# One up slab by eight products, another order of the first two slabs, and copies and joins ahead of splits, in a two-block transformer kernel

## The chip, the core and the metric

The kernel runs on one core of a Trainium2 chip. The metric is the device time of one execution in microseconds (us); lower is better. The engines are TensorE (PE; its weight loads are PEld), VectorE (DVE), ScalarE (ACT), GpSimd (POOL) and SyncE (SP, which here only issues DMAs). Each has its own in-order instruction queue, and they meet only at semaphores: an instruction that waits holds up everything behind it on its engine.

## The reference, cut to what matters

Two blocks are computed one after the other on 512 tokens of width 1024, all in float32. The change touches three products of them:

```python
# first block, entry
h = rmsnorm(x, norm_mix_pre); proj = h @ w_in          # the first two slabs of w_in
# first block, MLP (width 4096)
f = relu(h @ w_up) ** 2; y = f @ w_down
# second block, end
h = rmsnorm_2(x, norm_ffn_2)
x = x + (silu(h @ w_ffn_gate_2) * (h @ w_ffn_up_2)) @ w_ffn_down_2   # width 2816
```

## The kernel before

**Slabs.** Every weight matrix is read in slabs of 1024 x 256 (two column blocks of 128; 1 MB). Float32 accuracy is had by splitting each operand into a high and a low float32r part: ACT copies raw to `hi`, then DVE (for the first slab POOL) subtracts raw - hi into `lo`. A product is then three matmuls per 128 deep tile: hi by hi, hi by input-low, lo by input-hi. A slab by eight products is 2 blocks x 8 tiles x 3 = 48 matmuls of 512 tokens, summed in two of the four `gemm` banks (`G`).

**Seven products.** Most slabs of the MLP's up matrix (`up4` to `up15`) and of the second block's gate and up matrices (`fgate1`.. and `fup1`..) are multiplied in Strassen-Winograd form: seven products, each 4 pairs x 3 = 12 matmuls of 256 tokens, 84 in all, in the order 1, 6, 7, 5, 2, 4, 3. They go through the four `misc` banks (`M`) in turn, so product number n waits until the bank of number n-4 has been read (`p_read`). They need sums of weight quarters, made by POOL in four operations (`weight_sums`, `ffn_sums`), a split of the slab in three parts (`even`, `sums`, `odd`, each a `hi` on ACT and a `lo` on DVE), a copy of product 1 out of its bank (`copy_p1` on ACT), and seven joins on DVE (`join_u2`, `join_u3`, `join_u4_c22`, `join_c11_c21`, `join_c12`). For the gate slabs there follow a scaling by RSTD (`scale`), tanh on ACT, `silu` on DVE, another RSTD factor on POOL (`norm_gate`), and `gated` on DVE.

**Order.** Nothing is planned at run time: each engine's program is written out by hand, in the loop `for w in range(1, N_W)` for the second block's end. Slab numbers there, counted from `fgate0`: `fgate0` 0, `fup0` 1, `fgate1` 2, `fup1` 3, `fgate2` 4, `fup2` 5, then a down slab (`fpart2`) 6. Slabs 0 and 1 are done by eight products (`first_gate`, `up_block`), 2 to 5 by seven. A raw buffer (three of them) is loaded again when the slab three before is done, a `hi` buffer (two) is free when the slab two before is done, and the buffers of weight sums are two.

**Entry.** SP issues the four quarters of x and then slab 0 in two DMAs (columns 0 to 127 and 128 to 255). ACT squares x, copies two transposed tiles (L1527), waits for both halves of slab 0, makes `w_hi` in one operation (L1492, called as `split_hi(0)`) and then the eight `h_hi` tiles (L1500). POOL waits for `hi_done` and makes `w_lo` in eight operations (L3194), with one increment after the last. PE's `first_slab` (L671, L676) does 16 matmuls w_hi by h_hi in the order in which h_hi comes, waits for all of `w_lo`, does 16 w_lo by h_hi, then 16 w_hi by h_lo. DVE starts h_lo (L2271) when `w_lo` is there, and makes slab 1's low part behind it (`split_lo(1)`, L2212). Slab 1 is an ordinary `slab`: it waits for its low part before its first matmul.

**MLP.** For u in 4 to 15, ACT and DVE first make parts of the next slab and then copy and join products of slab u. `up14` is the one with another seven-product slab on both sides (`paired and closed`).

Of the kernel before, what the change touches and what calls it, by code (L numbers as in the profile page):

```python
# [25 lines left out]
P = 128  # L26
# [88 lines left out]
def build(nc, a, out):  # L115
# [115 lines left out]
    PIECES = [4 if PH["nsa"][0] + 3 <= s < PH["nsa"][0] + 5 else 3 if PH["branch2"][0] <= s < PH["branch2"][0] + 4 or s == PH["small"][0] else 2  # L231
# [191 lines left out]
    SEVENS = [W_SLAB[w] + n for w in range(1, N_W) for n in range(2)]  # L423
# [13 lines left out]
    def joined_at(n, x):  # L437

        return S("joined"), JOINED_0 + 8 * ((n + 1) // 2) + 7 * (n // 2) + x
# [33 lines left out]
    def _(sp):  # L473
# [158 lines left out]
    def _(pe):  # L632
# [26 lines left out]
        def first_slab(s, blocks, hi_base, lo_base):  # L659

            m = BLOCKS_BEFORE[s]
            pe.wait_ge(S("hi_done"), s + 1)
            for b in range(blocks):
                pe.wait_ge(evac[(m + b) % 4], (m + b) // 4 + 1)
            for w in (hi_of, lo_of):
                if w is lo_of:
                    pe.wait_ge(S("lo_done"), s + 1)
                for k in range(KT):
                    pe.wait_ge(S("hhi_ready"), hi_base + k + 1)
                    for b in range(blocks):  # L670
                        nc.tensor.matmul(G[(m + b) % 4][:], w(s)[:, k, P * b:P * b + P], HHI[:, k, :],  # L671
                                         start=k == 0 and w is hi_of, stop=False)
            for b in range(blocks):
                for k in range(KT):
                    pe.wait_ge(S("hlo_ready"), lo_base + k + 1)
                    mm = nc.tensor.matmul(G[(m + b) % 4][:], hi_of(s)[:, k, P * b:P * b + P], HLO[:, k, :],  # L676
                                          start=False, stop=k == KT - 1)
                mm.then_inc(S("block_full"), 1)

        def run(name, hi, lo, kts=range(KT), ready=None, lo_slab=0, slabs=None, new_h=None):  # L680
            s0, n, _, _ = PH[name]
            n = slabs or n
            for s in range(s0 + lo_slab, s0 + lo_slab + n):
                if new_h and s == s0 + lo_slab:
                    first_slab(s, 2, *new_h)
                else:
                    slab(s, hi, lo, kts, ready)
# [29 lines left out]
        pe.wait_ge(S("inv_ready"), 1)  # L717
# [53 lines left out]
        mm.then_inc(S("ln_var"), 1)  # L771
# [4 lines left out]
        mm.then_inc(S("ln_spread"), 1)  # L776
# [359 lines left out]
        for hd in range(GLA_H):  # L1136
            nc.tensor.matmul(take((hd + 1) % 4)[:], ONE32[32 * hd:32 * hd + 32, :], RS4[32 * hd:32 * hd + 32, :],
                             start=True, stop=True).then_inc(S("gla_rstd_full"), 1)
# [10 lines left out]
        mm.then_inc(S("hidden_full"), 1)  # L1149
# [240 lines left out]
        for w in range(1, N_W):  # L1390
            for n in (2 * w - 2, 2 * w - 1):
                for p in ORDER[1 if n == 0 else 0:]:
                    product(n, p)
# [72 lines left out]
    def _(act):  # L1466
# [49 lines left out]
        act.wait_ge(S("eps_ready"), 1)  # L1516
# [11 lines left out]
        split_hi(0)  # L1528
# [59 lines left out]
        act.wait_ge(S("ln_var"), 1)  # L1588
# [161 lines left out]
        for u in range(FIRST7, N_UP):  # L1750
            s = PH[f"up{u}"][0]
            paired, closed = s + 1 in UP_AT, s - 1 in UP_AT
            if paired:
# [3 lines left out]
            up_copy(u)  # L1757
# [192 lines left out]
        act.wait_ge(S("hidden_full"), 1)  # L1950
        A_(HT[:], M[2][:, 0:P], ACT.Tanh, scale=0.5).then_inc(S("hidden_tanh"), 1)
# [161 lines left out]
        def gate_tanh(w, b):  # L2113

            act.wait_ge(*joined_at(2 * w - 2, SCALED_AT))
            A_(SQ[b][:], FGATE[:, b, :], ACT.Tanh, scale=0.5).then_inc(S("ffn_tanh"), 1)

        def act_hi(w, b):

            if w:  # L2120
                act.wait_ge(S("ffn_gated"), 2 * w - 1 + b)
            else:
                act.wait_ge(*evac_at(PH["fup0"][2] + b))
# [7 lines left out]
        for w in range(1, N_W):  # L2131
            f_ = W_SLAB[w]
            even_hi(f_ + 1)
            copy_p1(2 * w - 2)
            if w <= 2:
                if w == 2:
                    act_hi(w - 1, 0)
                act_hi(w - 1, 1)
            sums_hi(f_ + 1)
            odd_hi(f_ + 1)  # L2140
            if f_ + 2 in SEVEN_OF:
                even_hi(f_ + 2)
# [54 lines left out]
    def _(dve):  # L2197
        V = nc.vector
        V.memset(EPSB[:], EPS).then_inc(S("eps_ready"), 1)
        for n in (128, 512):  # L2200
            V.memset(INV[n][:], 1.0 / n)
        V.memset(INV[1024][:], 1.0 / 1024).then_inc(S("inv_ready"), 1)
# [174 lines left out]
        dve.wait_ge(S("ln_spread"), 1)  # L2377
# [1036 lines left out]
```

## Time and profile before

| | us |
|---|---|
| median of 3 runs | 1400.23 (1400.18 to 1402.51) |
| the profiled execution's own time | 1401.67 |
| its span | 1399.5 |
| PE busy | 1379.1 (99% of the span) |
| DVE busy | 1020.1 (73%) |
| ACT busy | 615.1 (44%) |
| POOL busy | 419.4 (30%) |

The span is what the trace covers, from the first instruction to the last; the execution's own time is 2.2 us more. The TensorE clock granted was 0.998 of full over the span. Times in rows are counted from the span's start. A matmul's row has a start and a length; matmuls overlap, so the step from one start to the next is what one costs, not its length.

### The profile page before, as it was taken

Reading aid. Unit: us, or ns where it says so; the run is one execution under the profiler, and the core shown is the slowest. Engines: PE = TensorE matmul, PEld = TensorE weight load, DVE = VectorE, ACT = ScalarE, POOL = GpSimd, SP = SyncE. Lnnn points to the kernel's source line nnn. Section 1 sums busy time; section 2 is a strip of 40 time slices with the busy share of each in tenths; the row PEclk is TensorE's granted clock in tenths of the full one; section 3 lists DMA queues with packets and bytes.
Section 4 is the critical chain, followed back from the end, with each engine's and each line's share of the span. In section 5 each row is a group of like instructions: output and inputs, shape, how many; then the busy total and the mean of one; then the engine's idle time right before and its main releaser. Section 6 shows DMA issues by size and latency. Waiting matters only on the chain.

```text
span 1399.5 us, 20853 instructions
## 1 busy us (share of the span) xinstructions
PE 1379.1 (99%) x8375; PEld 1176.2 (84%) x8375; DVE 1020.1 (73%) x1490; ACT 615.1 (44%) x905; POOL 419.4 (30%) x311
## 2 busy tenths in 40 slices
PE   7999999999999999999999999999999999999998
PEld 6888788988988999888878776668888899999997
DVE  6998774757776687578474666774579999998983
ACT  6223344646333434346453437662355343433434
POOL 1040014101333234121132711111235654455532
PEclk9999999999999999999999999999999999999999
DMA  6322223303323323423244212111323232332322
GB/s 201 119 91 91 91 90 124 118 0 96 116 91 92 120 91 100 119 91 98 90 91 121 74 61 61 31 31 61 120 63 94 86 121 91 109 103 91 121 68 83
DMA packets 125792, 129.89 MB, mean 93 GB/s; under 512 B 15777, under 2 KB 110945, under 8 KB 125665
## 3 DMA queue, kind: packets, MB, share of 16 engines
q1 hardware_dynamic: 124560, 124.90, 28.5%
q0 software_dynamic: 992, 3.47, 0.8%
q8 instruction: 67, 1.10, 0.3%
q14 instruction: 29, 0.23, 0.0%
q10 hardware_dynamic: 144, 0.20, 0.0%
HBM read 126.06 MB, written 2.10 MB: 92 GB/s over the span
## 4 chain that ended last, share of the span: by engine, by line
PE 90%; DVE 4%; ACT 2%; issue 2%; POOL 1%; DMA 1%; SPq 0%; ACTq 0%; DVEq 0%; POOLq 0%
PE gemm L643 30%; PE misc L1314 13%; PE gemm L916 9%; PE misc L902 8%; PE gemm L1343 6%; PE gemm L762 3%; PE gemm L1219 2%; PE gemm L930 2%; PE gemm L1357 2%; PE misc L1240 2%; PE misc L1259 1%; PE gemm L846 1%; PE gemm L793 1%; PE gemm L1232 1%; PE misc L1067 1%
## 5 line engine op out<-in xcount | busy, mean ns | idle before, releaser
L643 PE MATMUL gemm<-h_hi,w_hi 128*128 128x512 f32 x520 | 205.0, 394 | 0.0
L643 PE MATMUL gemm<-h_hi,w_lo 128*128 128x512 f32 x520 | 202.5, 389 | 0.0
L643 PE MATMUL gemm<-h_lo,w_hi 128*128 128x512 f32 x520 | 202.5, 389 | 0.0
L2212 DVE TENSOR_TENSOR w_lo<-w_raw,w_hi 128x2048 fp32r<-128x2048 f32 x45 | 103.6, 2303 | 68.8 <-ACT w_hi L1492 68.7
L643 PEld LDWEIGHTS gemm<-h_hi,w_hi 128*128 128x128 f32 x520 | 97.6, 188 | 23.2 <-issue 2.4
L643 PEld LDWEIGHTS gemm<-h_hi,w_lo 128*128 128x128 f32 x520 | 97.6, 188 | 20.4
L643 PEld LDWEIGHTS gemm<-h_lo,w_hi 128*128 128x128 f32 x520 | 97.7, 188 | 19.9 <-issue 0.2
L1492 ACT ACTIVATE w_hi<-w_raw 128x2048 fp32r<-128x2048 f32 x50 | 95.5, 1910 | 5.4 <-PE gemm L762 3.2
L1314 PE MATMUL misc<-ffn_in_hi,ffn_hi 128*128 128x256 f32 x320 | 90.9, 284 | 4.2 <-ACT copy_p L2111 2.6
L1314 PE MATMUL misc<-ffn_in_lo,ffn_hi 128*128 128x256 f32 x320 | 90.5, 283 | 0.0
L1314 PE MATMUL misc<-ffn_in_hi,ffn_lo 128*128 128x256 f32 x320 | 90.5, 283 | 0.0
L2302 DVE SCALAR_TENSOR_TENSOR conv_out<-v_padded,conv_cols,conv_out 128x512 f32<-128x512 f32 x120 | 89.8, 807 | 0.5
L3242 POOL TENSOR_TENSOR mlp_sums<-mlp_raw 128x512 f32<-128x512 f32 x12 | 22.2, 1852 | 211.3 <-DMA mlp_raw<-in_w_up 202.9
L916 PE MATMUL gemm<-f_hi,mlp_hi 128*128 128x512 f32 x192 | 74.8, 389 | 0.0
L916 PE MATMUL gemm<-f_lo,mlp_hi 128*128 128x512 f32 x192 | 74.8, 389 | 0.0
L916 PE MATMUL gemm<-f_hi,mlp_lo 128*128 128x512 f32 x192 | 74.7, 389 | 0.0
L3229 POOL TENSOR_TENSOR sq_sum<-sq_sum,sq 128x512 f32<-128x512 f32 (+1 forms) x27 | 39.2, 1453 | 103.3 <-ACT sq L2029 51.4
L1314 PE MATMUL misc<-ffn_in_hi,ffn_sums_hi 128*128 128x256 f32 x240 | 68.1, 284 | 0.4 <-DVE ffn_up L3007 0.4
L2048 ACT ACTIVATE ffn_hi<-ffn_raw 128x1024 fp32r<-128x1024 f32 x20 | 21.2, 1061 | 106.7 <-POOL ffn_raw L3360 77.9
L1314 PE MATMUL misc<-ffn_in_lo,ffn_sums_hi 128*128 128x256 f32 x240 | 67.9, 283 | 0.0
L1314 PE MATMUL misc<-ffn_in_hi,ffn_sums_lo 128*128 128x256 f32 x240 | 67.9, 283 | 0.0
L3368 POOL TENSOR_TENSOR ffn_gate<-ffn_gate,rstd 128x512 f32<-128x512 f32 x20 | 30.8, 1557 | 119.1 <-DVE ffn_gate L3055 119.1
(608 smaller groups left out, 4058.2 us busy)
## 6 DMA issues: line engine op xcount, KB each, us to landing
w_raw<-in_w_in SPq DMA_DIRECT2D x62, 512.0 KB, 4.6
mlp_raw<-in_w_down SPq DMA_DIRECT2D x32, 512.0 KB, 4.6
mlp_raw<-in_w_up SPq DMA_DIRECT2D x26, 512.0 KB, 4.7
ffn_raw<-in_w_ffn_gate SPq DMA_DIRECT2D x22, 512.0 KB, 4.7
ffn_raw<-in_w_ffn_up SPq DMA_DIRECT2D x22, 512.0 KB, 4.4
ffn_raw<-in_w_ffn_down SPq DMA_DIRECT2D x16, 512.0 KB, 4.3
w_raw<-in_w_o SPq DMA_DIRECT2D x8, 512.0 KB, 4.0
w_raw<-in_w_out SPq DMA_DIRECT2D x8, 512.0 KB, 4.0
```

The costliest lines, as they stand in the source:

```text
L643: mm = nc.tensor.matmul(bank[:], w(s)[:, kt, col0:col0 + P], x(n), start=first, stop=last)
L762: mm = nc.tensor.matmul(G[m % 4][:], wide(w(s0 + j))[:, k, P * b:P * b + P], x[:, k, :], start=k == 0 and n == 0, stop=k == 3 and n == 2)
L902: mm = nc.tensor.matmul(up_bank(u, p)[:, 0:HALF], w, x, start=pair == 0 and n == 0, stop=pair == 3 and n == 2)
L916: mm = nc.tensor.matmul(G[m % 4][:], wide(w(s))[:, k, P * b:P * b + P], x(4 * c + k), start=k == 0 and n == 0, stop=k == 3 and n == 2)
L930: mm = nc.tensor.matmul(G[m % 4][:], w(s)[:, k, P * b:P * b + P], x(3 * KT + k), start=n == 0, stop=n == 23)
L1314: mm = nc.tensor.matmul(bank[:, 0:HALF], w_, x[:, a_, pair, :], start=pair == 0 and i == 0, stop=pair == 3 and i == 2)
L1343: mm = nc.tensor.matmul(G[m % 4][:], wide(w)[:, k, P * b:P * b + P], x[:, e, :], start=k == 0 and n == 0, stop=k == 3 and n == 2)
L1492: nc.scalar.activation(part(hi_of(s), s), part(raw_of(s), s), ACT.Copy).then_inc(S("hi_done"), SLABS_AT[s])
L2212: V.tensor_tensor(part(lo_of(s), s), part(raw_of(s), s), f(part(hi_of(s), s)), SUB).then_inc(S("lo_done"), SLABS_AT[s])
L2302: ins = V.scalar_tensor_tensor(y, x, w, y, MUL, ADD)
L3229: Q.tensor_tensor(SQA[:, cols], SQA[:, cols], SQ[j % 2][:, cols], ADD).then_inc(S("sq_added"), 1)
L3368: Q.tensor_tensor(FGATE[:, b, :], FGATE[:, b, :], RSTD[:], MUL).then_inc(S("gate_normed"), 1)
```

## The change

Four things, and a renaming of semaphores (`eps_ready`, `inv_ready` to `fills_ready`; `ln_var`, `ln_spread` to `ln_full`; `gla_rstd_full`, `hidden_full` to `late_full`; `r_tanh`, `hidden_tanh` to `branch_tanh`) with counts to match.

1. `fup1` is done by eight products (`up_block(1, 0)`, `up_block(1, 1)`, in `G` banks) instead of seven. POOL makes no sums for it, its split is one `down_hi` and one `down_lo` (whole slab), there are no joins for it; `first_silu` and `first_gated` take over for w = 1. The loops of ACT and DVE get a branch for w = 1 in which `copy_p1` comes ahead of the splits. On POOL the sums of `fgate2` come directly behind those of `fgate1`.
2. Slab 0: its first half has a semaphore of its own and a `w_hi` copy of its own; POOL increments after each low tile; PE takes the low products of tile k-1 right behind the high ones of tile k, and the h_lo products tile by tile for both blocks.
3. Slab 1 (`second_slab`): all products with w_hi first, for both blocks, those with w_lo last.
4. MLP: for `up4` the copy and the joins u2, u3 come ahead of the next slab's split; for `up14` the odd part's low split comes behind the joins c11 and c21.

```diff
-        FFN_PHASES += [(f"fgate{w}", 1, 0 if w else 2), (f"fup{w}", 1, 0 if w else 2)]
+        FFN_PHASES += [(f"fgate{w}", 1, 0 if w else 2), (f"fup{w}", 1, 0 if w > 1 else 2)]
...
-    SEVENS = [W_SLAB[w] + n for w in range(1, N_W) for n in range(2)]
+    SEVENS = [W_SLAB[w] + n for w in range(1, N_W) for n in range(2) if w + n != 2 or n == 0]
...
+            if c == 0:
+                dst, src = sides.pop(0)
+                sp.dma_start(dst, src).then_inc(S("first_side"), 16)
...
+        def first_slab():
+            def lows(k):
+                pe.wait_ge(*((S("first_lo"), k + 1) if k < KT - 1 else (S("lo_done"), 1)))
+                for b in range(2):
+                    nc.tensor.matmul(G[b][:], lo_of(0)[:, k, P * b:P * b + P], HHI[:, k, :], start=False, stop=False)
+            for k in range(KT):
+                pe.wait_ge(S("hhi_ready"), k + 1)
+                for b in range(2):
...
+                    nc.tensor.matmul(G[b][:], hi_of(0)[:, k, P * b:P * b + P], HHI[:, k, :], start=k == 0, stop=False)
+                if k:
+                    lows(k - 1)
+            lows(KT - 1)
+            for k in range(KT):
+                pe.wait_ge(S("hlo_ready"), k + 1)
+                for b in range(2):
+                    mm = nc.tensor.matmul(G[b][:], hi_of(0)[:, k, P * b:P * b + P], HLO[:, k, :], start=False, stop=k == KT - 1)
...
+        def second_slab():
+            pe.wait_ge(S("hi_done"), 2)
...
+            for w, x in ((hi_of, HHI), (hi_of, HLO), (lo_of, HHI)):
+                if w is lo_of:
+                    pe.wait_ge(S("lo_done"), 2)
+                for b in range(2):
+                    for k in range(KT):
...
-        split_hi(0)
+        act.wait_ge(S("first_side"), 16)
+        nc.scalar.activation(hi_of(0)[:, :, 0:P], raw_of(0)[:, :, 0:P], ACT.Copy).then_inc(S("first_hi"), 1)
+        act.wait_ge(*raw_full(0))
+        nc.scalar.activation(hi_of(0)[:, :, P:SLAB], raw_of(0)[:, :, P:SLAB], ACT.Copy).then_inc(S("hi_done"), 1)
...
@@ scalar, the second block's end @@
+            if w == 1:
+                copy_p1(GATE_N[w])
+                act_hi(0, 1)
+                down_hi(f_ + 1)
+                even_hi(f_ + 2)
+                gate_tanh(w, 0)
+                gate_tanh(w, 1)
+                sums_hi(f_ + 2)
+                odd_hi(f_ + 2)
+                act_hi(1, 0)
+                continue
...
@@ vector, MLP @@
+            if u == FIRST7:
+                up_u2(u)
+                up_u3(u)
...
-            if paired:
+            if paired and not closed:
                 up_odd_lo(u + 1)
             up_c11(u)
             up_c21(u)
+            if paired and closed:
+                up_odd_lo(u + 1)
...
@@ vector, the second block's end @@
+                first_gated(0, 1)
                 act_lo(0, 0)
+                join_u2(gate)
+                act_lo(0, 1)
+                join_u3(gate)
+                down_lo(f_ + 1)
+                join_u4_c22(gate)
+                join_c11_c21(gate)
+                join_c12(gate)
+                scale(w)
+                even_lo(f_ + 2)
+                first_silu(w, 0)
+                first_silu(w, 1)
+                sums_lo(f_ + 2)
+                first_gated(w, 0)
+                odd_lo(f_ + 2)
+                continue
+            if w == 2:
+                first_gated(1, 1)
+                act_lo(1, 0)
             even_lo(f_ + 1)
...
@@ gpsimd @@
-        ins.then_inc(S("lo_done"), 1)
+            ins.then_inc(S("first_lo") if k < KT - 1 else S("lo_done"), 1)
...
         weight_sums(0)
-        for w in range(1, N_W):
-            weight_sums(2 * w - 1)
-            if W_SLAB[w] + 2 in SEVEN_OF:
-                weight_sums(2 * w)
+        weight_sums(1)
+        for w in range(2, N_W):
+            weight_sums(UP_N[w])
```

## Rows read from the trace of the kernel before

**Rows 1.** The page, part 1: busy time of each engine, share of the span.
```profile
PE 1379.1 (99%) x8375; PEld 1176.2 (84%) x8375; DVE 1020.1 (73%) x1490; ACT 615.1 (44%) x905; POOL 419.4 (30%) x311
```
**Rows 2.** Timeline of the entry: start us, us, engine, line, what, [idle before <-releaser].
```profile
2.67 8.02 SPq L507 DMA_DIRECT2D w_raw<-in_w_in  x4
12.78 1.91 ACT L1492 ACTIVATE w_hi<-w_raw 128x2048 fp32r<-128x2048 f32 x1 [1.16 <-DMA w_raw<-in_w_in]
14.59 5.02 ACT L1500 ACTIVATE h_hi<-h_T 128x512 fp32r<-128x512 f32 x8
14.76 5.62 POOL L3194 TENSOR_TENSOR w_lo<-w_raw,w_hi 128x256 fp32r<-128x256 f32 x8 [13.82 <-ACT w_hi L1492]
15.35 5.05 PE L671 MATMUL gemm<-h_hi,w_hi 128*128 128x512 f32 x16 [2.52 <-ACT h_hi L1500]
20.41 4.90 DVE L2271 TENSOR_TENSOR h_lo<-h_T,h_hi 128x512 fp32r<-128x512 f32 x8 [1.47 <-POOL w_lo L3194]
20.43 3.93 PE L671 MATMUL gemm<-h_hi,w_lo 128*128 128x512 f32 x16
27.86 0.48 PE L643 MATMUL gemm<-h_hi,w_hi 128*128 128x512 f32 x1
```
**Rows 3.** DMA issues from 2.6 to 3.1 us: count, KB, us to landing.
```profile
w_raw<-in_w_in SPq DMA_DIRECT2D x1, 512.0 KB, 8.3
```
**Rows 4.** Timeline of ACT: one copy of 128x1024.
```profile
1048.99 1.05 ACT L2048 ACTIVATE ffn_hi<-ffn_raw 128x1024 fp32r<-128x1024 f32 x1
```
**Rows 5.** Timeline of PE: first and last of 48 matmuls, at 512 and at 256 tokens.
```profile
1037.04 0.39 PE L1368 MATMUL gemm<-ffn_in_hi,ffn_hi 128*128 128x512 f32 x1
...
1047.69 0.39 PE L1368 MATMUL gemm<-ffn_in_hi,ffn_lo 128*128 128x512 f32 x1
...
1060.55 0.28 PE L1314 MATMUL misc<-ffn_in_hi,ffn_hi 128*128 128x256 f32 x1
...
1066.18 0.28 PE L1314 MATMUL misc<-ffn_in_hi,ffn_sums_lo 128*128 128x256 f32 x1
```
**Rows 6.** Timeline of DVE: a whole slab's low part, that of slab 8.
```profile
97.68 2.28 DVE L2212 TENSOR_TENSOR w_lo<-w_raw,w_hi 128x2048 fp32r<-128x2048 f32 x1
```
**Rows 7.** Timeline of DVE and PE at the turn from up14 to up15.
```profile
557.43 1.21 DVE L2543 TENSOR_TENSOR mlp_lo<-mlp_raw,mlp_hi 128x1024 fp32r<-128x1024 f32 x1
...
559.11 0.36 PE L902 MATMUL misc<-mlp_in_sums_hi,mlp_sums_hi 128*128 128x256 f32 x1 [0.29 <-DVE relu L2548]
```
**Rows 8.** Timeline of PE, 1040 to 1110 us: all matmuls that waited.
```profile
1067.49 0.35 PE L1314 MATMUL misc<-ffn_in_hi,ffn_hi 128*128 128x256 f32 x1 [1.03 <-ACT copy_p L2111]
1084.27 0.35 PE L1314 MATMUL misc<-ffn_in_hi,ffn_sums_hi 128*128 128x256 f32 x1 [0.42 <-DVE ffn_up L3007]
1090.43 0.36 PE L1314 MATMUL misc<-ffn_in_hi,ffn_hi 128*128 128x256 f32 x1 [1.62 <-ACT copy_p L2111]
1094.39 0.35 PE L1314 MATMUL misc<-ffn_in_hi,ffn_hi 128*128 128x256 f32 x1 [0.64 <-DVE join_u L3007]
1096.88 0.36 PE L1314 MATMUL misc<-ffn_in_hi,ffn_hi 128*128 128x256 f32 x1 [0.83 <-DVE ffn_gate L3007]
```
**Rows 9.** Timeline of ACT around the first and third of these waits.
```profile
1065.49 0.63 ACT L2124 ACTIVATE ffn_act_hi<-ffn_up 128x512 fp32r<-128x512 f32 x1 [7.06 <-DVE ffn_up L3062]
...
1066.98 0.37 ACT L2111 ACTIVATE copy_p<-misc 128x256 f32<-128x256 f32 x1
...
1088.96 1.06 ACT L2048 ACTIVATE ffn_hi<-ffn_raw 128x1024 fp32r<-128x1024 f32 x1 [6.62 <-POOL ffn_raw L3360]
```
**Rows 10.** The page, part 6: a gate slab's DMAs, us to landing.
```profile
ffn_raw<-in_w_ffn_gate SPq DMA_DIRECT2D x22, 512.0 KB, 4.7
```
**Rows 11.** By line: duration ns min/median/max, first and last start us.
```profile
L3358 POOL TENSOR_TENSOR ffn_sums<-ffn_raw x20: 1290/1416/2677, 1043.0 to 1329.9; 128x512 f32<-128x512 f32 x20
L3048 DVE SCALAR_TENSOR_TENSOR ffn_gate<-sq,ffn_gate x2: 1776/1780/1783, 1057.8 to 1061.2; 128x512 f32<-128x512 f32 x2
L3055 DVE SCALAR_TENSOR_TENSOR ffn_gate<-sq,ffn_gate x20: 679/683/995, 1079.4 to 1351.0; 128x512 f32<-128x512 f32 x20
```

More of the change, by code:

```diff
@@ L422, in build @@
     W_SLAB = [PH[f"fgate{w}"][0] - SF for w in range(N_W)]
-    SEVENS = [W_SLAB[w] + n for w in range(1, N_W) for n in range(2)]
+    SEVENS = [W_SLAB[w] + n for w in range(1, N_W) for n in range(2) if w + n != 2 or n == 0]
+    GATE_N, UP_N = [[SEVENS.index(W_SLAB[w] + n) for w in range(2, N_W)] for n in range(2)]
+    GATE_N, UP_N = [None, 0] + GATE_N, [None, None] + UP_N
+    JOINS_TO = [sum(7 if x in UP_N else 8 for x in range(n)) for n in range(len(SEVENS))]
     SEVEN_OF = {f_: n for n, f_ in enumerate(SEVENS)}
@@ new lines, in second_slab @@
+        def second_slab():
+            pe.wait_ge(S("hi_done"), 2)
+            for b in range(2):
+                pe.wait_ge(evac[2 + b], 1)
+            for w, x in ((hi_of, HHI), (hi_of, HLO), (lo_of, HHI)):
+                if w is lo_of:
+                    pe.wait_ge(S("lo_done"), 2)
+                for b in range(2):
+                    for k in range(KT):
+                        mm = nc.tensor.matmul(G[2 + b][:], w(1)[:, k, P * b:P * b + P], x[:, k, :],
+                                              start=k == 0 and w is hi_of and x is HHI, stop=k == KT - 1 and w is lo_of)
+                    if w is lo_of:
+                        mm.then_inc(S("block_full"), 1)
@@ L681, in run @@
+        def run(name, hi, lo, kts=range(KT), ready=None, lo_slab=0, slabs=None):
             s0, n, _, _ = PH[name]
@@ L683, in run @@
             for s in range(s0 + lo_slab, s0 + lo_slab + n):
[L684 to L687, printed above, removed]
+                slab(s, hi, lo, kts, ready)
         def mean_rows(src, start, stop, bank=M[0]):
@@ L1137, in _ @@
             nc.tensor.matmul(take((hd + 1) % 4)[:], ONE32[32 * hd:32 * hd + 32, :], RS4[32 * hd:32 * hd + 32, :],
-                             start=True, stop=True).then_inc(S("gla_rstd_full"), 1)
+                             start=True, stop=True).then_inc(S("late_full"), 1)
         gate_block(3)
@@ L1390, in _ @@
         for w in range(1, N_W):
-            for n in (2 * w - 2, 2 * w - 1):
-                for p in ORDER[1 if n == 0 else 0:]:
-                    product(n, p)
+            for n in (GATE_N[w], UP_N[w]):
+                if n is None:
+                    up_block(1, 0)
+                    up_block(1, 1)
+                else:
+                    for p in ORDER[1 if n == 0 else 0:]:
+                        product(n, p)
             if 2 <= w < N_W - 1:
@@ L3009, in joined_into @@
         def joined_into(n):
-            return FUP if n % 2 else FGATE
+            return FUP if n in UP_N else FGATE
         def join_u2(n):
```

149 lines of the change are left out of this document (62 added, 87 removed).

## The prediction

> **What bounds the kernel now.** I read the page's part 1 first: PE is busy for 1379.1 of 1399.5 us and the next engine for 73% [rows 1]. So an edit pays only where it shortens PE's list of matmuls or takes away a stop of PE. Next I read what a matmul costs, as the step between starts: 48 matmuls of 512 tokens start within 47 steps from 1037.04 to 1047.69, so 0.2266 us each; at 256 tokens it is 47 steps from 1060.55 to 1066.18, 0.1198 us each [rows 5]. A slab by eight products is thus 48 x 0.2266 = 10.88 us and one by seven products 84 x 0.1198 = 10.06 us. Then I looked for PE's stops in the timeline, in the three places that the change touches.
>
> Entry: PE's first matmul of slab 0 is at 15.35, the first of slab 1 at 27.86; 48 matmuls take 12.5 us instead of 10.9, because the first 16 follow h_hi (5.05 us for 16) and the next 16 wait for the last of POOL's eight low tiles [rows 2]. MLP: one stop, at 559.11 [rows 7]. Second block's end: five stops between 1067 and 1097 [rows 8], and none after; they are the start-up of the seven-product pipeline.
>
> **Part A, entry.** ACT is free at 12.78 - 1.16 = 11.62 and waits until 12.78 for slab 0 [rows 2]. The first of its two DMAs is issued at 2.67 [rows 2] and lands 8.3 us later, at 10.97 [rows 3]. So the first half copy starts at 11.62, and takes 1.05 us [rows 4]; the second starts at 12.78, when the second DMA is there as before, and ends at 13.83. Before, the whole copy took 1.91 and h_hi began at 14.59; now h_hi 0 begins near 13.75 and POOL at 13.9 instead of 14.76 (0.86 earlier). The split in two costs ACT 0.2 us more, hidden in the 1.16 us of waiting; uncovered, it would be 0.2 us later. Later h_hi tiles gain less: the last ended at 19.61, and h_T comes from DVE; I give them 0.1 us.
>
> PE then: h_hi 0 is there at 14.4, so the start is 14.5. Each tile is now four matmuls, 0.91 us, slower than POOL's pace of 5.62/8 = 0.70 and h_hi's of 5.02/8 = 0.63 [rows 2]. Only tile 3 is late (h_hi 3 at about 16.97, where PE would be at 16.96), nothing else. Thirty-two matmuls are 7.25 us, with two small waits 22.0. Sixteen more follow with h_lo: 3.63 us, to 25.7. DVE starts h_lo when POOL is done, 13.9 + 5.62 = 19.5, and needs 4.90: the last at 24.5, PE wants it at 25.2. So slab 1 can start at 25.75 instead of 27.86: **2.1 us**. Bounds: if nothing comes earlier from ACT, PE starts at 15.35, waits 0.15 more for h_hi 1 and ends at 15.95 + 30 x 0.2266 + 3.63 = 26.4, a gain of 1.5; if there are no waits at all from 14.5, 14.5 + 10.88 = 25.4, a gain of 2.5.
>
> What would be late next is slab 1's low part: DVE makes it behind h_lo, until 24.5 + 2.3 = 26.8 (2.28 for such a part [rows 6]). The old order would have waited there 1.1 us; the new one has 32 matmuls with w_hi first and wants it at 33.0. Its first column block is complete 16 x 0.2266 = 3.6 us later than before, its second at the same point; the ACT and DVE work behind it on their queues waits for the second anyway. Farther on DVE runs the convolution, and its low parts come on time by about 4 us: that of slab 8 is done at 97.68 + 2.28 = 99.96, while PE reaches slab 8 at 27.86 + 7 x 10.88 = 104.0 [rows 2, 5, 6]. A PE that is 2.1 us earlier doesn't use that up. No stop takes the gain back.
>
> **Part B, MLP.** At up15's second product PE stood for DVE's join of up14; ahead of that join lay the odd low part, 1.21 us from 557.43 [rows 7]. Moved behind two joins, it is done at 559.3, and up15's product 2 wants it at 563. The stop is gone: 0.29 by its row, 0.45 us against the pace. I take **0.45**, ends 0.2 and 0.5. The same edit for up4 costs and gives nothing: it puts a whole split (1.9 on ACT, 2.28 on DVE) behind the third product, and the four products that are left (5.8 us) cover it; without that cover it would cost up to its 2.28 us of low part.
>
> **Part C, second block's end.** Matmuls: 10.88 instead of 10.06, so +0.82 us. Stops: I follow PE from 1066.30, when product 5 of fgate1 has been issued.
>
> - Copy of product 1: ACT made the act_hi tile until 1066.12, then the even part for fup1, then the copy [rows 9]. Now the copy comes second, done at 1066.4. PE resumes at 1066.55 instead of 1067.49 and ends fgate1 (three products, 4.32 us) at 1070.9.
> - fup1 needs one low part of the whole slab. ACT copies it from 66.95 to 68.85 (1.9). On DVE the low part (2.28) stands behind act_lo 0, u2, act_lo 1, u3. Here POOL matters. fgate2's raw slab may be loaded when fup0 is done, 1060.55, and lands 4.7 after its issue [rows 5, 10], so POOL's four sums start at about 1065.4 and no longer at 1072. In the rows, the DVE product of two SBUF tiles takes 0.68 us when alone (L3055) and 1.78 when it ran beside POOL (L3048), and a POOL sum 1.29 at best and up to 2.68 [rows 11]. Taken in turns, each waits for the other's whole operation, some 1.1 to 1.2 us. In turns I get act_lo 0 at 67.2, act_lo 1 at 68.95, POOL's third sum to 70.15, the low part to 72.3. PE starts fup1 at 72.4: a new stop of 1.5 us. It ends at 83.3.
> - In these 10.9 us DVE does five joins (0.33 each), two scalings, fgate2's even low part, four silu steps and the sums' low part (1.75): 74.0, 75.2, 76.4, then in turns with POOL's sums for fup2 (its raw slab lands at about 75.4) silu to 83.4, sums to 85.1. fgate2's second product wants this at 84.75: a stop of 0.45. Its product 1 copy, stood before behind fup2's even high part, and this behind POOL's sums for fup2, made late (ACT idle 6.62 until 1088.96 [rows 9]). They are now made by about 1079 to the part that it needs: the 1.62 stop is gone. The joins u2 (89.6) and u3 (90.5) come before 90.9 and 92.4, C22 (92.95) before 93.8.
> - fgate2 so takes 10.06 + 0.45, from 83.3 to 93.85, where fup2 started at 1096.88 [rows 8]. **3.0 us** earlier, with the 0.82 in it.
>
> Bounds: no collisions between DVE and POOL, then fup1 starts at 1071.2, fup2 at 1092.1, gain 4.8. If the three last stops of [rows 8], 3.1 us by the rows, stay for want of DVE time, the gain is zero to 0.5. Nothing that is queued later gets more work.
>
> The collision itself is also what the Trainium skill says ("SBUF — State Buffer", Who interferes with whom): a DVE instruction with two SBUF inputs and a GpSimd instruction that reads SBUF exclude each other for their whole length, and which was issued first decides. The rows agree (1.78 against 0.68 us). Read without it, the sum of part C would be 4.8, with it 3.0.
>
> **Sum.** 2.1 + 0.45 + 3.0 = 5.55 us. The profiled execution took 1401.67, so it would be 1396.1; this is 1.44 above the median of 1400.23, and the median after is then 1394.7.
>
> **Rivals.**
>
> 1. *No collisions.* POOL's earlier sums fall into DVE's waits; C is 4.8, the sum 7.35, time 1392.9. For it: the joins, with one operand in PSUM, don't collide. Against: the four silu steps lie just where fup2's sums run.
> 2. *The stops move on.* in my working of part C DVE has no idle time at all from 1066 to 1094, so any slip goes to PE; fup1's start and fgate2's second and fifth products wait as long as the old ones: C is 0.5, sum 3.0, time 1397.2.
> 3. *The entry doesn't pass on.* The convolution on DVE takes its slack back, or h_hi is no earlier: A is 0 to 0.5, sum 3.7, time 1396.5. Against: 4 us of slack.
> 4. *Slower.* DVE's silu chain ahead of fgate2's `sums_lo`: if each of the five POOL operations beside it holds DVE for its longest 2.68 us (instead of about 1.15), the sums come 5 x 1.53 = 7.65 us later, at 1092.75, PE stops 8.0 instead of 0.45, and C is -4.55: sum -2.0, time 1402.2. It decides from 5.55 us of lateness, 2.3 us per POOL operation. Against: 2.68 contains POOL's own waiting, and 1.29 is its length alone [rows 11].
>
> **How the numbers follow.** Forecast 50%, rival 1 20%, rival 2 14%, rival 3 11%, rival 4 5%. Range: the forecast's own bounds are 1393.5 to 1396; toward both sides I go to 1392.0 (rival 1 with the entry's better end) and 1397.8 (rival 2 with the worse). A measurement of this kernel tells 0.2% (2.8 us) from no change: faster than 1397.4 are the forecast, rivals 1 and 3, and half of rival 2, 0.88, of which I keep 0.86; within, half of rival 2 and part of rival 4: 0.11; slower 0.03.
>
> **What would show it.** Slab 1's first matmul at 25.75 (25.4 to 26.4), the first of slab 0 near 14.5. No wait at up15. fup1 (then `up_block`) starting 1.5 us after fgate1's last product, behind DVE's whole low part; fgate2's second product behind the sums' low part; fup2 starting 3.0 us earlier relative to fup0's end. Sections between them with unchanged lengths. It would be wrong if a stop longer than 0.5 us appeared in the convolution stage, or if the stops in fgate2 were still over 3 us.

## The result, and the profile after

| us | before | after |
|---|---|---|
| median | 1400.30 (1400.18 to 1402.51, 4 runs) | 1391.61 (1391.17 to 1392.80, 4 runs) |
| the profiled execution's own time | 1401.67 | 1391.79 |
| its span | 1399.5 | 1389.9 |
| first matmul of slab 1 | 27.86 | 26.37 |
| first matmul of `up4` | 337.45 | 335.95 |
| first matmul of `fgate1` | 1060.55 | 1056.94 |
| first down matmul (L1343, after L1367) | 1107.05 | 1098.07 |
| start of the last nine matmuls | 1392.78 | 1383.99 |

The ratio is 0.9936, 95% interval [0.9918, 0.9953]: 9.0 us less (6.6 to 11.5), where 5.55 was forecast and 1392.0 was the lower end of the range. (The medians of the table differ by 8.7.) In the text below, "us less" beside a ratio is what the ratio makes of 1400. Busy times after, from the page's part 1 [rows 1]:

```profile
PE 1375.9 (99%) x8339; PEld 1173.7 (84%) x8339; DVE 1015.8 (73%) x1483; ACT 614.0 (44%) x903; POOL 404.6 (29%) x305
```

**Where the 9.9 us between the two profiled executions went.** I take PE's position from one stage to the next. Up to slab 1 it gained 1.49 us, though in this execution the setup data landed 0.55 later (PE's first matmul at 5.44 instead of 4.89), so the entry itself is 2.04 shorter. The convolution added 0.01. The MLP gave 0.52. Between 816 and 820 us there are 1.57 us that no edit gave: the kernel before ran there at a granted clock of 0.57, that after at 1.00 (see the last section). From `fgate1` to the first down matmul it is 46.50 before and 41.13 after, 5.37 less, of which a later stage takes 0.19 back. From the last matmuls to the end of the span it is 0.8 less, and 0.3 lies outside the spans. The edits' own part is thus 2.04 + 0.52 + 5.18 = 7.7 us.

That the entry may be counted from PE's first matmul is borne out by the other traces. Where the clock was full, the five with the new entry have 20.84 to 20.93 us from there to slab 1, though the first matmul stood anywhere from 4.90 to 5.97. The traces with the old entry have 22.97 (the kernel before) and 22.61 (the second block's end alone), so the 2.04 is 1.7 to 2.1.

Entry, timelines of ACT, POOL, DVE and PE after; the columns are as in [rows 2]:

```profile
11.77 1.06 ACT L1557 ACTIVATE w_hi<-w_raw 128x1024 fp32r<-128x1024 f32 x1
12.95 1.06 ACT L1559 ACTIVATE w_hi<-w_raw 128x1024 fp32r<-128x1024 f32 x1
14.18 1.95 ACT L1528 ACTIVATE h_hi<-h_T 128x512 fp32r<-128x512 f32 x3 [0.17 <-DVE h_T L2304]
16.88 3.27 ACT L1528 ACTIVATE h_hi<-h_T 128x512 fp32r<-128x512 f32 x5 [0.76 <-DVE h_T L2304]
...
14.08 5.63 POOL L3247 TENSOR_TENSOR w_lo<-w_raw,w_hi 128x256 fp32r<-128x256 f32 x8 [13.14 <-ACT w_hi L1559]
...
24.57 2.28 DVE L2249 TENSOR_TENSOR w_lo<-w_raw,w_hi 128x2048 fp32r<-128x2048 f32 x1
...
22.71 3.79 PE L687 MATMUL gemm<-h_lo,w_hi 128*128 128x512 f32 x16
26.34 0.27 PE L747 MATMUL misc<-setup_rows 124*128 124x124 f32 x1
26.37 0.94 PE L701 MATMUL gemm<-h_hi,w_hi 128*128 128x512 f32 x3
```

h_hi comes in two groups. Tiles 4 to 8 wait for DVE's h_T and end at 20.15 (before: 19.61, with the setup data 0.55 sooner), so they gained nothing; PE has the low products to do meanwhile.

The second block's end after: the boundaries on PE, then what DVE and POOL did in `fgate1` and `fup1`. None of these matmuls carries a bracket: nothing waited.

```profile
1056.94 0.28 PE L1338 MATMUL misc<-ffn_in_hi,ffn_hi 128*128 128x256 f32 x1
...
1067.01 0.40 PE L1352 MATMUL gemm<-ffn_in_hi,ffn_hi 128*128 128x512 f32 x1
...
1077.92 0.28 PE L1338 MATMUL misc<-ffn_in_hi,ffn_hi 128*128 128x256 f32 x1
...
1098.07 0.40 PE L1367 MATMUL gemm<-ffn_act_hi,ffn_hi 128*128 128x512 f32 x1
```

```profile
1054.21 0.68 DVE L3092 SCALAR_TENSOR_TENSOR ffn_gate<-sq,ffn_gate 128x512 f32<-128x512 f32 x1
1054.93 0.69 DVE L3094 TENSOR_TENSOR ffn_gate<-ffn_gate,rstd 128x512 f32<-128x512 f32 x1
...
1058.00 1.28 DVE L3106 TENSOR_TENSOR ffn_up<-ffn_gate,gemm 128x512 f32<-128x512 f32 x2
...
1061.97 2.29 DVE L3001 TENSOR_TENSOR ffn_lo<-ffn_raw,ffn_hi 128x2048 fp32r<-128x2048 f32 x1
...
1072.68 1.78 DVE L3092 SCALAR_TENSOR_TENSOR ffn_gate<-sq,ffn_gate 128x512 f32<-128x512 f32 x1
1074.50 1.66 DVE L3094 TENSOR_TENSOR ffn_gate<-ffn_gate,rstd 128x512 f32<-128x512 f32 x1
1076.09 2.84 DVE L2990 TENSOR_TENSOR ffn_sums_lo<-ffn_sums,ffn_sums_hi 128x1536 fp32r<-128x1536 f32 x1
...
1062.57 2.85 POOL L3411 TENSOR_TENSOR ffn_sums<-ffn_raw 128x512 f32<-128x512 f32 x1 [17.68 <-DMA ffn_raw<-in_w_ffn_gate]
...
1072.47 1.45 POOL L3411 TENSOR_TENSOR ffn_sums<-ffn_raw 128x512 f32<-128x512 f32 x1 [2.71 <-DMA ffn_raw<-in_w_ffn_up]
```

The reader is to see two things. The collisions that I forecast are there (1.78, 1.66 and 2.84 for operations that take 0.68, 0.69 and 1.75 alone). But the first silu, at 1054.21, took 0.68 where it took 1.78 before [rows 11], and the pair of `first_gated` products begins 1.06 us after `fgate1`'s first matmul. Before, it began 4.23 after it:

```profile
1054.04 2.68 POOL L3358 TENSOR_TENSOR ffn_sums<-ffn_raw 128x512 f32<-128x512 f32 x1 [5.20 <-DVE ffn_in_sums L2970]
1056.80 2.25 POOL L3360 TENSOR_TENSOR ffn_raw<-ffn_raw 128x512 f32<-128x512 f32 x1
...
1064.78 1.28 DVE L3062 TENSOR_TENSOR ffn_up<-ffn_gate,gemm 128x512 f32<-128x512 f32 x2
```

These POOL operations of the kernel before are the sums for `fup1`, which the change takes out. After the change, the low part for `fup1` was done at 1064.3, 2.8 us before PE wanted it.

### The profile page after: what moved, and what is told of

Same layout as the page of the kernel before. It is cut to its first block, busy times and chain, and to the rows that moved or that the text cites. A ratio compares the mean times of both kernels' runs of the same rounds, so it can differ in the third digit from the quotient of the medians.

```text
span 1389.9 us, 20753 instructions
## 1 busy us (share of the span) xinstructions
PE 1375.9 (99%) x8339; PEld 1173.7 (84%) x8339; DVE 1015.8 (73%) x1483; ACT 614.0 (44%) x903; POOL 404.6 (29%) x305
## 4 chain that ended last, share of the span: by engine, by line
PE 96%; DVE 1%; ACT 1%; issue 1%; DMA 0%; ACTq 0%
PE gemm L650 30%; PE misc L1338 14%; PE gemm L940 9%; PE misc L926 9%; PE gemm L1367 6%; PE gemm L786 3%; PE gemm L1243 3%; PE gemm L954 2%; PE gemm L1381 2%; PE misc L1264 2%; PE gemm L1352 2%; PE misc L1283 1%; PE gemm L870 1%; PE gemm L817 1%; PE gemm L701 1%; PE gemm L1392 1%
## 5 line engine op out<-in xcount | busy, mean ns | idle before, releaser
L650 PE MATMUL gemm<-h_hi,w_hi 128*128 128x512 f32 x504 | 198.7, 394 | 0.0
L650 PE MATMUL gemm<-h_hi,w_lo 128*128 128x512 f32 x504 | 196.3, 389 | 0.0
L650 PE MATMUL gemm<-h_lo,w_hi 128*128 128x512 f32 x504 | 196.3, 389 | 0.0
L1338 PE MATMUL misc<-ffn_in_lo,ffn_hi 128*128 128x256 f32 x304 | 86.0, 283 | 0.0
L1338 PE MATMUL misc<-ffn_in_hi,ffn_lo 128*128 128x256 f32 x304 | 86.0, 283 | 0.0
L1338 PE MATMUL misc<-ffn_in_hi,ffn_hi 128*128 128x256 f32 x304 | 86.0, 283 | 0.0
L1338 PE MATMUL misc<-ffn_in_hi,ffn_sums_hi 128*128 128x256 f32 x228 | 64.6, 283 | 0.0
L1338 PE MATMUL misc<-ffn_in_hi,ffn_sums_lo 128*128 128x256 f32 x228 | 64.5, 283 | 0.0
L1338 PE MATMUL misc<-ffn_in_lo,ffn_sums_hi 128*128 128x256 f32 x228 | 64.5, 283 | 0.0
L2540 DVE TENSOR_TENSOR y_T<-y_T,gemm 128x512 f32<-128x512 f32 x46 | 31.4, 683 | 42.6 <-PE gemm L940 30.0
```

The lines of the kernel that those rows point to most:

```text
L650: mm = nc.tensor.matmul(bank[:], w(s)[:, kt, col0:col0 + P], x(n), start=first, stop=last)
L1338: mm = nc.tensor.matmul(bank[:, 0:HALF], w_, x[:, a_, pair, :], start=pair == 0 and i == 0, stop=pair == 3 and i == 2)
L2540: V.tensor_tensor(y, y, G[m % 4][:], ADD).then_inc(evac[m % 4], 1)
```

## The experiments

A useful measure beside the time is the *end stage*: from `fgate1`'s first matmul to the first down matmul, 46.50 us before, 41.13 after. Without a stop it would be 3 x 10.06 + 10.9 = 41.1. A stop *against the pace* is the step from one matmul's start to the next, less the normal step (0.12 us at 256 tokens, 0.23 at 512). One execution's time moves by more than a microsecond for reasons of the clock, so for effects of that size the stage or stop in the trace decides, and the ratio only confirms. The first four kernels ran on one chip, the next four on a second, the last four on a third; across chips the ratios are compared, each to the kernel before on the same chip, and not the times.

**The kernel after again.**

> The changed kernel again, for the size of the whole. From the two traces: entry 2.0 us (1.5 seen, with x's first data 0.55 later in that execution), MLP 0.5, second block's end 5.2, together 7.7 us; the rest of the 8.7 measured (a half-clock stretch of 1.6 us that only the profiled execution of before had, and the last stores landing 0.8 sooner) is taken as chance. If so: 7.7 us less than before, plus or minus 0.5. If something steady is hidden in the rest: 8.5 or more.

1392.64, ratio 0.9943 [0.9930, 0.9955], 8.0 us less. End stage 41.14. The size of the edits' own part, 7.7, holds; this median would have been inside the forecast's range.

**The entry alone** (the kernel before, with slab 0 in halves and interleaved, `second_slab`, and the semaphore names).

> The kernel before with the entry's edits alone (slab 0 in halves, interleaved low weights, slab 1 with w_lo last) and the renamed semaphores. Theory: 2.0 us less than before, slab 1's first matmul 11.5 us after PE's first transpose of x (13.0 before). Rival 3 of the prediction (the entry doesn't pass on): 0 to 0.5 us.

1399.16, ratio 0.9989 [0.9981, 0.9998], 1.5 us less. From PE's first matmul to slab 1 it is 20.91 us, as in the kernel after, so the entry gives what it should. But the MLP takes some of it back (in the profiled execution 0.9 of the 1.0 us that PE was ahead in place):

```profile
PE misc L923 <- DVE up_u L2572: 0.7, 1, 0.7
```

This is PE's list of waits (total, times, longest). The wait is at 344.67, in `up4`, 0.9 us against the pace. In the kernel before the join it waits for was just in time, 0.3 us ahead. PE now comes 1.0 us sooner and DVE does not (the join u2 starts at 344.11, before at 343.94).

**The second block's end alone** (the kernel before, with the `FFN_PHASES`, `SEVENS` and w = 1 edits).

> The kernel before with the second block's end changed alone. Theory (all five stops go and none comes): 6.0 us of stops less 0.82 of matmuls, 5.2 us less than before. The forecast as put: 3.0. If the rest in e0 belongs to this part: 6.

1395.06, ratio 0.9954 [0.9941, 0.9968], 6.4 us less. End stage 41.13, the same as with all edits: it does not depend on the entry.

**GpSimd busy again beside the first silu** (the kernel after; four additional subtractions whose results are overwritten):

```diff
         weight_sums(0)
+        pool.wait_ge(*ffn_raw_full(3))
+        pool.wait_ge(S("ffn_in_part"), PARTS_0 + 4)
+        for i in (0, 1, 2, 0):
+            gstep.inc(Q.tensor_tensor(sums_of(1)[0][:, i, :, :].rearrange("p a n -> p (a n)"), XT[:, 2 * i, :], XT[:, 2 * i + 1, :], SUB))
+            gstep.wait(pool)
         weight_sums(1)
```

> The changed kernel, with four more GpSimd operations of the size and at the place of fup1's weight sums (they subtract tiles of x into the buffer of sums, which is overwritten afterwards). Theory: what the prediction missed is that without fup1's sums GpSimd stands idle beside first_silu, so VectorE reaches fup0's first_gated 3.2 us earlier relative to fgate1's first product. With the four operations back, the silu steps take 1.7 to 1.8 us again, and the stops of the forecast come (1.5 at fup1's start, 0.3 at the copy, 0.5 at fgate2's second product): 2 us more than the changed kernel. Rival (the whole gain is in the other order of ScalarE and VectorE, GpSimd doesn't matter): 0 to 0.3 us more.

1394.02, ratio 0.9951 [0.9938, 0.9963], 1.4 us more than the kernel after beside it (1392.64), where 2 was expected; the intervals overlap, and the trace decides. Timelines of DVE and PE:

```profile
1053.88 1.78 DVE L3092 SCALAR_TENSOR_TENSOR ffn_gate<-sq,ffn_gate 128x512 f32<-128x512 f32 x1
...
1067.97 0.50 PE L1352 MATMUL gemm<-ffn_in_hi,ffn_hi 128*128 128x512 f32 x1 [0.83 <-DVE ffn_lo L3001]
...
1081.25 0.39 PE L1338 MATMUL misc<-ffn_in_hi,ffn_sums_hi 128*128 128x256 f32 x1 [0.64 <-DVE ffn_sums_lo L2990]
```

The silu is back at 1.78, and the stops stand where the prediction had put them: the copy (0.23 us against the pace; forecast 0.25), `fup1`'s start (0.99; 1.5) and `fgate2`'s second product (0.80; 0.45). The end stage is 43.46, 2.3 more than after the change. Against the 46.50 before it is 3.04 less: with POOL busy at this place, part C gives the 3.0 of the forecast.

**GpSimd's sums for `fup1` cut short** (the kernel before, seven products kept; it leaves out most columns of these sums, so that `fup1`'s product is no longer the reference's, but every matmul is still done).

```diff
+            wide_ = 1 if n == 1 else P
+            if n == 1:
+                gstep.inc(Q.memset(t[:], 0.0))
+                gstep.wait(pool)
+            t = t[:, :, :, 0:wide_]
-            b11, b12, b21, b22 = (raw[:, k:KT:2, c:c + P] for k in range(2) for c in (0, P))
+            b11, b12, b21, b22 = (raw[:, k:KT:2, c:c + wide_] for k in range(2) for c in (0, P))
```

> The kernel before, with fup1 still by seven products, but GpSimd's four sums of fup1's weight quarters cut to one column in 128 (a memset of the buffer ahead of them), so that nothing of any length runs on GpSimd beside the first silu. Most columns of these sums, and with them part of fup1's product, are not computed. Theory (the time that part C was wrong by came from these four sums, which held DVE in the first silu): the two silu steps ahead of the first gated tile take 0.68 us each and no longer 1.78, the tile is begun 2.5 to 3.2 us sooner against fgate1's first product, the stop at product 1's copy in fgate1 (1.2 us against the pace) is gone, and of the four later stops (4.8 us together) the DVE ones shrink: 3 to 4.5 us less in all. Rival (what freed the second block's end is that fup1 needs no joins and no sums split, as the prediction had it): the stop at the copy goes at most, 1.2 us less, and the others stand where they were.

1398.43, ratio 0.9986 [0.9977, 0.9995], 2.0 us less. The silu and the pair of gated products on DVE:

```profile
1060.48 0.69 DVE L3048 SCALAR_TENSOR_TENSOR ffn_gate<-sq,ffn_gate 128x512 f32<-128x512 f32 x1
...
1064.28 1.28 DVE L3062 TENSOR_TENSOR ffn_up<-ffn_gate,gemm 128x512 f32<-128x512 f32 x2
```

The pair begins 1.06 us after `fgate1`'s first matmul (1063.22), exactly as in the kernel after, and the first two stops of [rows 8] and a small one between them are gone but for 0.13 (before: 1.19 + 0.20 + 0.58). The last three stand as they were, on PE's list of waits:

```profile
PE misc L1314 <- ACT copy_p L2111: 1.6, 1, 1.6
PE misc L1314 <- DVE ffn_gate L3007: 0.8, 1, 0.8
PE misc L1314 <- DVE join_u L3007: 0.6, 1, 0.6
```

So the theory is right for the first two stops and wrong for the last three: I had expected 3 to 4.5 us in all, which leaves 1 to 2.5 for them, and they gave nothing. The end stage is 44.52.

**Copy and join ahead of the split, alone** (the kernel before, seven products and all sums kept).

```diff
+            if w == 1:
+                copy_p1(0)
             even_hi(f_ + 1)
-            copy_p1(2 * w - 2)
+            if w > 1:
+                copy_p1(2 * w - 2)
... (and join_u2 ahead of even_lo in the same way)
```

> The kernel before, with fup1 still by seven products and GpSimd's sums as before; only the copy of fgate1's product 1 and its first join go ahead of the even split. Theory: the order at the copy is worth little as long as DVE is late by the silu: the stop in fgate1 shrinks to 0.1 to 0.4 us from 1.2, but DVE and ACT have the same work until fup2, so the later stops take most of it back: 0 to 0.5 us less in all. Rival (the order is what counts): 1.0 to 1.2 us less, all later stops of unchanged length.

1400.99, ratio 0.9999 [0.9990, 1.0008]. The stop at the copy fell from 1.19 to 0.24, and three others took its place: 0.20 at `fgate1`'s last product, 0.82 at `fup1`'s first (before: 0.20) and 0.82 at its second. The last three of [rows 8] stood as they were. The order by itself is worth nothing; the end stage is 47.00, even 0.5 longer.

**The copy behind the split** (the kernel after).

```diff
             if w == 1:
-                copy_p1(GATE_N[w])
                 act_hi(0, 1)
                 down_hi(f_ + 1)
+                copy_p1(GATE_N[w])
```

> The changed kernel, with ScalarE's order at fgate1 turned back: the second high tile of the gated product and the high part of fup1's slab first, the copy of fgate1's product 1 behind them. Theory (DVE is 3.2 us sooner at the first gated tile, so ScalarE has room): the copy is made about 2.6 us later, near 1062.0, PE needs its bank at about 1062.6: no stop, or one under 0.3 us; no change of the time (within 0.5 us). The joins u2 and what follows on DVE start later by up to 1.5 us, and fup1's low part ends near 1065.5, still ahead of 1067.0. Rival (the copy's place is what took away the 1.2 us stop at this point): a stop of 1 us or more comes back, and the time is 1 us longer.

1394.23, ratio 0.9952 [0.9939, 0.9964]. No stop at the copy, as the theory had it, but the end stage is 42.60, 1.5 longer (the ratio is too coarse for that). The stop is 20 us farther on:

```profile
1081.88 0.39 PE L1338 MATMUL misc<-ffn_in_hi,ffn_sums_hi 128*128 128x256 f32 x1 [1.21 <-DVE ffn_sums_lo L2990]
```

The silu steps of `fgate1` began 0.7 us later on DVE, met one more of POOL's operations (a second 1.70 instead of 0.69), and the sums' low part ended 1.7 us later. The kernel after has 0.4 us to spare there. Both of my theories looked at the copy only.

**Without the edit of `up4`** (the kernel after, `up_copy`, `up_u2` and `up_u3` back behind the split).

> The changed kernel without its edit of up4: there the split of the next slab stands again ahead of the copy and of the joins u2 and u3. Theory (PE comes to up4 1.5 us earlier by the entry, DVE and ScalarE do not, and the old order had just enough): one stop of 1.0 to 1.5 us at up4's sixth product, behind the join u2, near 344 us, and 1 us more of time. Rival (the prediction's: the edit costs and gives nothing, the four products that are left cover the split): no stop over 0.2 us, and the same time.

1393.69, ratio 0.9948 [0.9935, 0.9962], no different from the kernel after's 0.9943. The trace shows the stop that was expected. PE, with a step of 1.01 us instead of 0.12:

```profile
342.55 0.28 PE L926 MATMUL misc<-h_hi,mlp_lo 128*128 128x256 f32 x1
343.56 0.36 PE L926 MATMUL misc<-h_hi,mlp_last_sum_hi 128*128 128x256 f32 x1 [0.73 <-DVE up_u L2582]
```

`up4` takes 11.16 us instead of 10.07 (in the entry alone also 11.16). The prediction's "costs and gives nothing" was wrong by 1.1 us: the edit guards the entry's gain.

**Sums of `fgate2` at their old time** (the kernel after).

```diff
         weight_sums(0)
+        pool.wait_ge(*slab_done(SEVENS[0]))
         weight_sums(1)
```

> The changed kernel, with GpSimd's sums of fgate2's weights held back until fgate1's last product (10.07 us after its first), as in the kernel before; they ran from 5.6 us after it. Theory (the last three stops of the kernel before, 3.6 us, came from GpSimd's late queue and not from VectorE's lateness, so eight products of fup1 pay by letting GpSimd start early): the sums end 4 to 5 us later, the even and sums parts of fgate2 on ScalarE and VectorE follow them, and stops come back at fgate2's second product and at fup2's start, 1 to 2.5 us in all; fgate1's low part for fup1 has no collision any more. Rival (the early start only adds collisions, as the prediction priced it, and is worth nothing): no stop, the same time, or a little less.

1397.64, ratio 0.9972 [0.9960, 0.9984] instead of 0.9943, so 4.1 us more; the end stage is 45.87, 4.7 more. I had expected 1 to 2.5. All four silu steps now meet POOL (1.78, 1.68, 1.77, 1.67), and the sums' low part ends at 1083.5:

```profile
1080.70 2.81 DVE L2990 TENSOR_TENSOR ffn_sums_lo<-ffn_sums,ffn_sums_hi 128x1536 fp32r<-128x1536 f32 x1
...
1083.57 0.58 PE L1338 MATMUL misc<-ffn_in_hi,ffn_sums_hi 128*128 128x256 f32 x1 [3.12 <-DVE ffn_sums_lo L2990]
1083.95 0.42 PE L1338 MATMUL misc<-ffn_in_lo,ffn_sums_hi 128*128 128x256 f32 x1
```

(The last row is of the product's second matmul.) The stop is 3.28 us, and 1.5 more is lost behind it, while the granted clock is at its lower level (last section). So the early start is worth most of part C, not nothing.

But the last three stops of [rows 8] did not come back, though `fgate2`'s sums were late. What had made them lies elsewhere on POOL. Its timeline before, and with the sums late:

```profile
1080.49 4.43 POOL L3368 TENSOR_TENSOR ffn_gate<-ffn_gate,rstd 128x512 f32<-128x512 f32 x2 [0.63 <-DVE ffn_gate L3055]
1084.89 2.27 POOL L3358 TENSOR_TENSOR ffn_sums<-ffn_raw 128x512 f32<-128x512 f32 x1
```

```profile
1075.09 1.74 POOL L3411 TENSOR_TENSOR ffn_sums<-ffn_raw 128x512 f32<-128x512 f32 x1
```

These are the first sums for `fup2`. Before, the program lets them start only when `fup1` is done (1082.25, the buffers of sums are two), and the two `norm_gate` operations lie ahead of them; they ended 32.2 us after `fgate1`'s first matmul. With `fup1` by eight products neither holds: they ended at 24.0 here and at 23.2 in the kernel after.

**Slab 0's high part in one copy** (the kernel after).

> The changed kernel with slab 0's high part made in one copy when both halves have landed. Theory (the first h_hi tiles come 0.8 us later, but from the fourth on they follow VectorE's h_T, and GpSimd's eight low tiles end near 20.4 instead of 19.7): PE's first matmul of slab 0 0.7 to 0.85 us later, the small stops behind it (0.6 us together) gone, slab 1's first matmul 0.2 to 0.5 us later. Rival (all of the earlier start is passed on): slab 1 0.7 to 0.85 us later.

1394.03, ratio 0.9949 [0.9933, 0.9966]. Slab 0's second half lands at a time that differs from one execution to the next, so I count from it, against the kernel after run again: PE's first matmul 2.48 us after it instead of 1.74, slab 1 at 13.57 (27.24 - 13.67) instead of 13.23 (26.42 - 13.19). Of 0.74 us, 0.34 is passed on. Counted from PE's first matmul it is 0.6 (21.50 against 20.91), so which of the two it is depends on the landing that one takes.

**No interleaving** (the kernel after, all 16 products with w_hi first).

```diff
-                if k:
-                    lows(k - 1)
-            lows(KT - 1)
+            for k in range(KT):
+                lows(k)
```

> The changed kernel with the two half copies, but all 16 products w_hi by h_hi first and then the 16 with w_lo. Theory (the 16 follow the h_hi tiles, of which the last is there near 19.7; nothing else is there to do for PE meanwhile): stops of 1.2 to 1.5 us within the first 16, no stop at the low ones, slab 1's first matmul 0.5 to 1.0 us later. Rival (the gain of the entry came from the earlier start alone, 0.5 of it from the half copy): the same start of slab 1 within 0.2 us.

1393.88, ratio 0.9941 [0.9926, 0.9956]: times can't tell this one. The trace can:

```profile
14.68 1.96 PE L680 MATMUL gemm<-h_hi,w_hi 128*128 128x512 f32 x6 [1.59 <-ACT h_hi L1527]
17.30 3.37 PE L680 MATMUL gemm<-h_hi,w_hi 128*128 128x512 f32 x10 [0.65 <-ACT h_hi L1527]
20.50 1.78 PE L672 MATMUL gemm<-h_hi,w_lo 128*128 128x512 f32 x7
```

PE begins as early as after the change, but the low products begin at 20.50 (before: 20.43 [rows 2]), and slab 1 at 27.83 (before: 27.86). From PE's first matmul to slab 1 it is 22.67, inside the 22.61 to 22.97 of the old entry: the half copies alone give nothing that shows. The interleaving on top of them gives 1.5 us in place and 1.7 counted from each execution's first matmul (20.93), more than the 0.5 to 1.0 that I had expected.

**Slab 1 in the old order** (the kernel after, `slab(1, ...)` for `second_slab()`).

> The changed kernel with slab 1 in the old order, which waits for all of its low part ahead of the first matmul. The low part is done at 26.85 in the changed kernel and PE is free at 26.37. Theory: PE starts slab 1 at 26.9 to 27.0 instead, 0.5 us later, and passes all of it on to the end. Rival (the prediction's number, low part at 26.8 and PE at 25.75, so 1.1 us): over 0.9 us.

1393.12, ratio 0.9936 [0.9921, 0.9950]. Inconclusive: in the profiled execution the clock was at its lower level from 15 to 18 us, PE came to slab 1 only at 27.39, and the low part was there at 26.97. Where PE is there at 26.37, as after the change, the old order would wait some 0.5 us; that was not seen.

## Why the prediction was wrong, step by step

Of the 3.4 us between 5.55 and 9.0, 2.2 are part C. Parts A and B together were right within 0.1; the last 1.3 lie inside the interval of the measurement (6.6 to 11.5), and the kernel after run again gave 8.0.

- **Part A, entry: right in size, in part by luck.** Forecast 2.1, trace 2.04 (1.49 net of the later setup), by the other traces 1.7 to 2.1. In the kernel after, PE's first matmul of slab 0 is at 14.86 (14.5) and slab 1 at 26.37 (25.75, range 25.4 to 26.4). In the trace without the edit of `up4`, whose setup data landed as early as before, they are 14.25 and 25.74: PE starts 0.25 sooner than forecast and loses 0.6 in small stops instead of 0.4, and the two misses cancel. The later h_hi tiles gained nothing, as I had nearly assumed; it is the interleaving that uses the wait. That the convolution takes nothing back held (0.01 us). The low part of slab 1 was done at 26.85, as forecast (26.8).
- **Part B, MLP: right for `up14`/`up15`** (0.45 forecast, 0.52 measured, the stop of [rows 7] gone), **wrong for `up4`**. The step was "the four products that are left cover it". I counted PE's time and not where DVE stood. With PE 1.0 us earlier (the entry alone) and 2.1 (without this edit), `up4` is 1.1 us longer. The edit is in the change, so this did not enter the sum; without it part A would have lost half. That the stop of [rows 7] went by the edit of `up14` is borne out by the two kernels without it, the entry alone and the end alone, which have the stop.
- **Part C: the step that failed.** It is "In turns I get act_lo 0 at 67.2", which starts from ACT's act_hi tile, 1065.49 to 1066.12 in the old trace [rows 9], and with it the "new stop of 1.5 us", the 0.45 and the 0.25. I had kept DVE's position from the trace before although the change removes the four POOL sums that had made it late. Rows 11 held the sign: the two L3048 products at 1.78 us stood between 1057.8 and 1061.2, beside the POOL operations that go (their rows are in the section on the result). Without them DVE is 3.2 us sooner, and the three stops of 2.2 us together are not there: 3.0 + 2.2 = 5.2, measured 5.37 less 0.19. Putting POOL's work back gives these stops again, in the same three places, 2.0 us together, and brings part C down to 3.04; taking it from the kernel before moves DVE by the same 3.2.
- **Right in part C:** the last three stops of [rows 8] went, and `fup2`'s sums come sooner, both as forecast ("by about 1079", measured 1080.1). They are not DVE's lateness by the silu: with `fup1`'s sums cut short DVE was 3.2 sooner, and all three stood. Nor are they the time of `fgate2`'s sums: held back, these cost 4.7, as one stop at `fgate2`'s second product, and the three stayed away. What is left is `fup2`'s own sums, behind `fup1`'s end and `norm_gate`; that is read from the program and the rows ([rows 9] for the first of the three), and no run took it away alone.
- **Rivals.** *No collisions* had the nearest time (1392.9) for a wrong reason: the collisions are there, 1.78 us against 0.68 alone; only the lateness that they cause was bought back upstream. The Trainium skill ("SBUF — State Buffer", Who interferes with whom) says that such a DVE operation and one of POOL exclude each other, and the trace agrees. *The stops move on* is what the order alone does (end stage 47.00). *The entry doesn't pass on* happens in part where `up4` is not edited. *Slower* did not happen: no step of the silu chain took over 1.78 us, and the sums' low part ended 0.4 before PE wanted it.
- **Range.** I took 4.8 as part C's best case. The end stage's 46.50 us less four seven-product slabs of 10.06 [rows 5] are 6.3 of stops; less the 0.82 of additional matmuls, a stage without a stop gives 5.4. An end of a range has to be that. By its own sum the prediction's lower end was also 1392.5 (1392.9 less the entry's 0.4) and not 1392.0; neither holds the 1391.61. None of its signs of being wrong could have caught this miss: they looked for longer stops only.

## What to carry to other kernels

When a change removes work from a helper engine, first read what ran beside that work and how long it took there against its shortest row; move that engine forward in time, and only then place the new waits. An edit that makes the bounding engine earlier needs, at every later place with little to spare, the position of the engine that feeds it, not the count of work that is left. Where a measured stage has only stops to lose, take its length without any as the end of the range.

## What the runs showed of the hardware that was not expected

The granted TensorE clock goes to its lower level (1.2 of 2.4 GHz) for some microseconds, in some executions and not in others. Three places:

- 816 to 820 us: granted 0.57 before, 1.00 after, 0.51 in the kernel after run again. The stretch from L1161 (L1185) to the next slab took 4.43, 2.86 and 5.17 us. Between the two traces of the kernel after this is 2.3 of the 3.1 us of span. The lower level stands near this place in seven of the fourteen traces. PE was not idle ahead of it: it had just issued 64 small matmuls, at the same pace in an execution that lost the clock (before) and in one that kept it (after):

```profile
812.30 3.76 PE L1189 MATMUL misc<-k_cmp,q_raw 64*128 64x31 f32 x64
```

```profile
810.29 3.76 PE L1213 MATMUL misc<-k_cmp,q_raw 64*128 64x31 f32 x64
```

- 14 to 18 us: 1.00 before and after, 0.62 with slab 1 in the old order, where PE had been busy for 1.75 of the 3 us from 9 to 12 instead of 2.95. The 32 matmuls up to h_lo took 8.99 us instead of 7.85. Yet with 2.60 of these 3 us one trace kept the clock (no interleaving), and with 2.63 another lost it from 16.3 us on (copy and join ahead). What decides is open.
- Behind a long stop. With the sums held back PE stood 3.3 us up to 1083.57, and the windows that follow show (from, to, length, busy PE, PEld, DVE, ACT, POOL, clock, DMA share, GB/s):

```profile
1082.00:1084.00 2.00, 0.43 (x2) 0.43 (x3) 2.00 (x2) 0.00 (x0) 0.00 (x0) 0.82 0.79 306
1084.00:1086.00 2.00, 2.00 (x11) 2.00 (x11) 2.00 (x4) 1.85 (x4) 0.00 (x0) 0.50 0.00 0
1086.00:1088.00 2.00, 2.00 (x16) 2.00 (x15) 2.00 (x4) 2.00 (x3) 0.00 (x0) 0.83 0.00 0
```

The first step behind the stop was 0.38 and the next thirteen 0.21 instead of 0.12. A stop of 3.3 us so cost 4.8; the stops of up to 1.8 in the kernel before show no such tail.
